# A hybrid diffusion block on one core: a new order of the modulation stage, and a Fourier stage on folded tokens

## The reference

```python
mod_x = silu(c) @ w_ada + b_ada                      # shift, scale, gate: 3 x 2048
mod_c = silu(c_ctx) @ w_ada + b_ada
h_x = rmsnorm(x, g_pre) * (1 + sc_x) + sh_x
h_c = rmsnorm(ctx, g_pre) * (1 + sc_c) + sh_c
xa, ba, ca, za, u, zb, f, zc, gl = split(h_x @ w_in)
u_c = h_c @ w_in[:, u columns]
...                                                  # conv branch, state-space branch
def fourier_mix(f):                                  # 4 groups of 256 channels
    fg = f.reshape(1, 512, 4, 256)
    return fft2(fg, axes=(1, 3), norm='ortho').real.reshape(1, 512, 1024)
yc = ((fourier_mix(f) @ fourier_w) * silu(zc)) @ proj_c
m = g0 * ya + g1 * yb + g2 * yc                      # g = sigmoid(gl)
out = x + gate * rmsnorm(m @ w_out, g_post)
```

## Time and profile before

| | |
|---|---|
| median of 3 runs | 2119.97 us (2119.87 to 2121.78) |
| the profiled execution | 2119.78 us, its span 2118.0 us |
| TensorE busy | 2051.6 us, 97% of the span |
| DVE busy, ACT busy | 1086.1 us (51%), 586.1 us (28%) |
| modulation stage | 0 to 166 us |
| Fourier stage | 1484.5 to 1542.5 us |

### The profile page before, as it was taken

One profiled execution on the slowest core, in us unless ns is written; L12 is line 12 of the kernel. 1 busy time (PEld: TensorE's weight loads), 2 busy tenths in 40 slices (PEclk: granted clock), 3 DMA queues, 4 the chain that ended last, 5 costly groups with the idle time before them and its releaser, 6 DMA issues.

```text
span 2118.0 us, 26445 instructions
## 1 busy us (share of the span) xinstructions
PE 2051.6 (97%) x9915; PEld 1667.9 (79%) x9915; DVE 1086.1 (51%) x1596; ACT 586.1 (28%) x816; POOL 27.3 (1%) x16
## 2 busy tenths in 40 slices
PE   3999999999999999999999999999999999999996
PEld 0578888888888788888888888888588888888885
DVE  5445898888888545554333444332343333333333
ACT  4325233333333322222222222222122222222231
POOL 0003100000000000000000000000000000000000
PEclk9999999999999999999999999999999999999998
DMA  9873533343333544443334444444033333334423
GB/s 371 309 217 112 171 101 100 92 104 98 104 99 108 165 125 141 128 136 106 99 97 134 141 131 125 126 132 146 10 94 95 100 99 91 97 99 158 169 93 116
DMA packets 384830, 272.16 MB, mean 128 GB/s; under 512 B 24804, under 2 KB 349900, under 8 KB 382916
## 3 DMA queue, kind: packets, MB, share of 16 engines
q1 hardware_dynamic: 374416, 267.04, 40.9%
q10 hardware_dynamic: 10356, 4.35, 1.5%
HBM read 253.25 MB, written 18.09 MB: 128 GB/s over the span
## 4 chain that ended last, share of the span: by engine, by line
PE 80%; DVE 9%; DMA 4%; ACT 2%; ACTq 2%; issue 2%; SPq 0%; DVEq 0%
PE ac L704 20%; PE ac L705 20%; PE ac L708 20%; ACTq L1090 2%; DVE S L1549 2%; DMA M<-Tl 1%; PE ss L879 1%; PE ac L878 1%; PE ac L879 1%; PE ss L880 1%; PE ac L880 1%; PE ss L878 1%; ACT S L894 1%; DMA wslot<-w_in 1%; PE ac L845 1%
## 5 line engine op out<-in xcount | busy, mean ns | idle before, releaser
L1448 DVE TENSOR_TENSOR wlo<-wslot,whi 128x1024 fp32r<-128x1024 f32 x310 | 379.6, 1225 | 647.9 <-ACT whi L894 643.8
L894 ACT ACTIVATE whi<-wslot 128x1024 fp32r<-128x1024 f32 x328 | 347.1, 1060 | 1253.2 <-PE ac L708 1034.4
L704 PE MATMUL ac<-hxh,whi 128*128 128x512 f32 x1664 | 652.3, 392 | 0.0
L705 PE MATMUL ac<-hxl,whi 128*128 128x512 f32 x1664 | 648.0, 389 | 0.0
L708 PE MATMUL ac<-hxh,wlo 128*128 128x512 f32 x1664 | 411.1, 389 | 0.9 <-DVE wlo L1448 0.9
L704 PEld LDWEIGHTS ac<-hxh,whi 128*128 128x128 f32 x1664 | 312.4, 188 | 67.8 <-issue 3.1
L708 PEld LDWEIGHTS ac<-hxh,wlo 128*128 128x128 f32 x1664 | 312.3, 188 | 66.1 <-DVE wlo L1448 1.3
L705 PEld LDWEIGHTS ac<-hxl,whi 128*128 128x128 f32 x1664 | 312.5, 188 | 64.3 <-issue 0.2
L704 PE MATMUL ac<-bah,whi 128*128 128x512 f32 x384 | 149.4, 389 | 0.0
L705 PE MATMUL ac<-bal,whi 128*128 128x512 f32 x384 | 149.4, 389 | 0.0
L708 PE MATMUL ac<-bah,wlo 128*128 128x512 f32 x384 | 94.8, 389 | 0.0
(11 more groups left out here) (316 smaller groups left out, 2135.7 us busy)
## 6 DMA issues: line engine op xcount, KB each, us to landing
wslot<-w_in SPq DMA_DIRECT2D x224, 512.0 KB, 3.9
ring<-w_ada SPq DMA_DIRECT2D x64, 512.0 KB, 8.0
gwt<-w_ada SPq DMA_DIRECT2D x128, 128.0 KB, 2.4
wslot<-w_out SPq DMA_DIRECT2D x32, 512.0 KB, 3.6
wslot<-proj_a SPq DMA_DIRECT2D x16, 512.0 KB, 4.1
wslot<-proj_b SPq DMA_DIRECT2D x16, 512.0 KB, 4.0
wslot<-proj_c SPq DMA_DIRECT2D x16, 512.0 KB, 3.9
xn<-x SPq DMA_DIRECT2D x4, 1024.0 KB, 8.8
```

The source lines that it names most:

```text
L704: mm(ac[:, bank, :], w, xh, start=(v == 0 and q == 0), stop=False)
L705: mm(ac[:, bank, :], w, xl, start=False, stop=False)
L894: cp = lambda o, i, scale=1.0: nc.scalar.activation(o, i, ACT.Copy, scale=scale)
L1448: tt(wlo[:, s, :], wslot[:, s, :], whi[:, (U0[k] + j) % 2, :].bitcast(F32), ALU.subtract)\
```

## The change

Modulation stage: c and c_ctx are loaded first on SP's queue into `crow` and transposed alone; the other vectors are transposed behind `ada(3)`. On ACT's queue lam and log_dt come first. All these buffers leave the place of `whi`. DVE takes the token scales behind the sine, puts the zero-order hold (`zoh`) into quarter 0 and the powers (`chunk_powers`) behind it. Pieces of `w_ada` are spread between x and context pieces, SP issues weight units and ctx between pieces, and in DVE's loop each `low` comes before the next `modulate`.

Fourier stage: cosines are even and sines odd about token 256. As each `fT` tile appears, DVE folds it: token t plus token 512-t goes to `fP` (with token 0), their difference stays in `fT`; token 256 is treated apart (`p256`, with the signs `alt`). `channels` multiplies the sums with the cosine columns and the differences with the sine columns; `tokens` makes 257 cosine and 256 sine results of 256 folded tokens. The mix forms both halves of the 512 tokens, the second half written in reverse; ACT casts the high parts. Tables shrink to 1283 columns.

```diff
-V_BADA, V_GPRE, V_CONV, V_C, V_CC, V_END = 0, 32, 48, 72, 88, 104
+V_BADA, V_GPRE, V_CONV, V_END = 0, 32, 48, 72
...
-    r = Region(whi_at)
+    r = Region(abr_at + 4 * TC * 4)
+    crow = r("crow", [2 * KD, 128])
     vrow = r("vrow", [V_END, 128])
     lam = r("lam", [128, 2, P])
     ldt = r("ldt", [128, 1])
     zt = [r(f"zt{i}", [128, P]) for i in range(8)]
     ei = r("ei", [128, P], I32)
-    assert r.p <= hxl_at
+    assert r.p <= abr_at + KD // 2 * TC * 4
...
-    dftt = at("dftt", [128, 2, TT, T], bal_at)
+    dftt = at("dftt", [128, 5 * HT + 3], bal_at)
+    cosT = dftt[:, 0:2 * HT + 2].rearrange("p (k c) -> p k c", k=2)
+    sinT = dftt[:, 2 * HT + 2:4 * HT + 2].rearrange("p (k c) -> p k c", k=2)
+    alt = dftt[:, 4 * HT + 2:5 * HT + 3]
+    fP = at("fP", [128, KW, HT], bal_at + KW * T * 4 - KW * HT * 4)
...
+    p256 = at("p256", [FG, FG, FGW // 2 + 1], bal_at + 5152)
+    p256n = at("p256n", [FG, 128], bal_at + 5152 + 2080)
...
+        for n, src in enumerate((c[0:1, :], c_ctx.rearrange("(a n) -> a n", a=1))):
+            sp.dma_start(crow[n * KD:(n + 1) * KD, :], src.rearrange("a (r p) -> (a r) p", p=128)).then_inc(cv_in, 16)
         for t in range(TT):
             sp.dma_start(xn[:, t, :], x[0, t * 128:(t + 1) * 128, :]).then_inc(x_in[t], 16)
-        for n in range(8):
+        for n in range(32):
             ada_unit(n)
-            if n == 5:
-                first_unit(0)
-                first_unit(1)
-        for t in range(CT):
-            sp.dma_start(cn[:, t, :], ctx[0, t * 128:(t + 1) * 128, :]).then_inc(c_in, 16)
-        for q in range(1, 4):
-            for r in range(8):
-                ada_unit(8 * q + r)
-                if r == 3:
-                    first_unit(2 * q)
-                    first_unit(2 * q + 1)
+            if n % 8 >= 6:
+                first_unit(n // 8 * 2 + n % 2)
+            if n in (8, 9):
+                sp.dma_start(cn[:, n - 8, :], ctx[0, (n - 8) * 128:(n - 7) * 128, :]).then_inc(c_in, 16)
...
-        pe.wait_ge(vec_in, 96)
-        tr(ss[:, 0, 0:V_END], vrow[:, :], ident[0:V_END, 0:V_END])
-        tr(ss[:, 1, 0:G], drow[:, :, :].rearrange("n l h -> n (l h)"), ident[0:G, 0:G]).then_inc(vec_ps, 1)
+        pe.wait_ge(cv_in, 32)
+        tr(ss[:, 0, 0:2 * KD], crow[:, :], ident[0:2 * KD, 0:2 * KD]).then_inc(cv_ps, 1)
...
+            if n == 3:
+                pe.wait_ge(vec_in, 64)
+                tr(ss[:, 1, 0:V_END], vrow[:, :], ident[0:V_END, 0:V_END])
+                tr(ss[:, 1, 128:128 + G], drow[:, :, :].rearrange("n l h -> n (l h)"), ident[0:G, 0:G]).then_inc(vec_ps, 1)
         turn(0, 0)
         cols(0)
         for n in range(1, 4):
             turn(0, n)
+        for r in range(4):
+            x_piece(0, r, range(4))
+            ada(8 + r)
+        ada(12)
+        turn(0, 4)
+        ada(13)
+        turn(0, 5)
+        ada(14)
         for q in range(3):
-            for r in range(4):
-                ada(8 * q + 8 + 2 * r)
-                ada(8 * q + 9 + 2 * r)
-                x_piece(q, r, range(4))
-                if r // 2 == (0 if q else 1):
-                    turn(q, 4 + r % 2)
+            if q:
+                x_piece(q, 0, range(4))
+                ada(8 * q + 12)
+                x_piece(q, 1, range(4))
+                turn(q, 4)
+                ada(8 * q + 13)
+                x_piece(q, 2, range(4))
+                ada(8 * q + 14)
+                turn(q, 5)
+                x_piece(q, 3, range(4))
+            ada(8 * q + 15)
+            c_piece(q, 0)
             cols(q + 1)
-            for r in range(4):
+            turn(q + 1, 0)
+            for r in range(1, 4):
                 c_piece(q, r)
+                if q < 2:
+                    ada(8 * q + 15 + r)
                 turn(q + 1, r)
+            if q < 2:
+                ada(8 * q + 19)
...
+            pe.wait_ge(fold_done, 2 * gr + 2)
+            for t in range(2):
+                for parts, c0, c1 in ((fP, 0, 129), (fT[:, :].rearrange("p (k t) -> p k t", t=T), 129, FGW)):
+                    for q in range(2):
+                        last = mm(ss[:, gr, t * FGW + c0:t * FGW + c1], parts[:, 2 * gr + q, t * 128:(t + 1) * 128],
+                                  dftw[:, q, c0:c1], start=(q == 0), stop=(q == 1))
+            last.then_inc(p_ps, 1)
+
+        def tokens(gr):
+            pe.wait_ge(p_cp, gr + 1)
+            b = 2 * (gr % 2)
             if gr >= 2:
+                pe.wait_ge(ac_free[b], A0[6] // 4 + 1)
+            for t in range(2):
+                mm(ac[:, b, 0:HT + 1], pp[:, gr, t, 0:128], cosT[:, t, :], start=(t == 0), stop=False)
+            mm(ac[:, b, 0:HT + 1], p256[0:FG, gr, 0:128], alt[0:FG, :], start=False, stop=True).then_inc(pw_done, 1)
+            if gr >= 2:
+                pe.wait_ge(ac_free[b + 1], A0[6] // 4 + 1)
+            for t in range(2):
+                last = mm(ac[:, b + 1, 0:HT], pp[:, gr, t, 128:FGW], sinT[:, t, :], start=(t == 0), stop=(t == 1))
+            last.then_inc(pw_done, 1)
+
+        for gr in range(FG):
+            if gr == FG - 1:
+                pe.wait_ge(fold_done, KW)
+                middle = fT[:, :].rearrange("p (g q t) -> p g q t", q=2, t=T)
                 for q in range(2):
+                    last = mm(ac[0:FG, 3, 0:129], middle[:, :, q, HT], dftw[:, q, 0:129], start=(q == 0), stop=(q == 1))
+                last.then_inc(tok_ps, 1)
+            channels(gr)
+        pe.wait_ge(tok_cp, 2)
         for gr in range(FG):
+            tokens(gr)
+            if gr == 0:
+                pe.wait_ge(p_cp, FG)
+                for t in range(2):
+                    mm(ss[:, 0, 0:HT + 1], p128[:, t, :], cosT[:, t, :], start=(t == 0), stop=False)
+                mm(ss[:, 0, 0:HT + 1], p256n[:, :], alt[0:FG, :], start=False, stop=True).then_inc(y128_ps, 1)
...
+        for i, src in enumerate((lam_re, lam_im)):
+            act.dma_start(lam[:, i, :], src[0].rearrange("d g p -> (d g) p")).then_inc(ssm_in, 16)
+        act.dma_start(ldt[:, :], log_dt[0].rearrange("d (g a) -> (d g) a", a=1)).then_inc(ssm_in, 16)
+        for rr, src in ((V_BADA, b_ada[0:1, 0:2 * D]), (V_GPRE, g_pre[0:1, :]), (V_CONV, conv_w)):
             n = src.shape[0] * src.shape[1] // 128
             act.dma_start(vrow[rr:rr + n, :], src.rearrange("a (r p) -> (a r) p", p=128)).then_inc(vec_in, 16)
         act.dma_start(drow[:, :, :], ssm_d.rearrange("a (n h) -> (a n) h", h=H).unsqueeze(1).to_broadcast([G, L, H]))\
            .then_inc(vec_in, 16)
-        for i, src in enumerate((lam_re, lam_im)):
-            act.dma_start(lam[:, i, :], src[0].rearrange("d g p -> (d g) p")).then_inc(ssm_in, 16)
-        act.dma_start(ldt[:, :], log_dt[0].rearrange("d (g a) -> (d g) a", a=1)).then_inc(ssm_in, 16)
-        act.wait_ge(vec_cp, 1)
-        a(small[:, 0:32], vecs[:, V_C:V_END], ACT.Sigmoid).then_inc(sg_done, 1)
+        act.wait_ge(cv_ps, 1)
+        a(small[:, 0:32], ss[:, 0, 0:32], ACT.Sigmoid).then_inc(sg_done, 1)
...
-        act.wait_ge(zn_done, 1)
+        high(0, 0)
         hi_first(0)
-        high(0, 0)
+        high(0, 1)
+        high(0, 2)
         hi_first(1)
-        for n in range(1, 4):
-            high(0, n)
+        high(0, 3)
...
+        for gr in range(FG):
+            if gr == FG - 1:
+                act.wait_ge(tok_ps, 1)
+                for g in range(FG):
+                    last = cp(p256[:, g, :], ac[0:FG, 3, 0:129], ident[0:FG, g:g + 1])
+                last.then_inc(tok_cp, 1)
+                act.wait_ge(tok_cp, 1)
+                cp(p256n[:, :].rearrange("p (g c) -> p g c", c=32)[:, :, 0], p256[:, :, 128]).then_inc(tok_cp, 1)
+            act.wait_ge(p_ps, gr + 1)
+            half = ss[:, gr, :].rearrange("p (t c) -> p t c", c=FGW)
+            cp(pp[:, gr, :, 0:128], half[:, :, 0:128])
+            cp(pp[:, gr, :, 129:FGW], half[:, :, 129:FGW])
+            cp(p128[:, :, 32 * gr:32 * gr + 1], half[:, :, 128:129]).then_inc(p_cp, 1)
+        for gr in range(FG):
+            act.wait_ge(pw_done, 2 * gr + 1)
             if gr:
+                act.wait_ge(gs_free, gr)
+            cp(gsig[:, 0:HT + 1], ac[:, 2 * (gr % 2), 0:HT + 1]).then_inc(ac_free[2 * (gr % 2)], 1)
+            for n, y in enumerate((gt, gtm2)):
+                act.wait_ge(mix_y, 2 * gr + n + 1)
+                cp(b2nd[:, 2 * gr + n, 0, :], y[:, :]).then_inc(mix_hi, 1)
...
             modulate(q, 0)
+            low(q, 0)
             modulate(q, 1)
-            low(q, 0)
+            low(q, 1)
             lo_first(2 * q)
             modulate(q, 2)
-            low(q, 1)
+            low(q, 2)
             modulate(q, 3)
-            low(q, 2)
+            low(q, 3)
             lo_first(2 * q + 1)
-            low(q, 3)
             if q == 0:
+                zoh()
                 token_scale(TT, CT, 2)
-            modulate(q, 4)
-            low(q, 4)
-            modulate(q, 5)
-            low(q, 5)
+            for n in range(4, 6):
+                modulate(q, n)
```

(80 more changed lines are left out.)

97 lines of the change are left out of this document (36 added, 61 removed).

## The result

The changed kernel took 2101.19 us (median of four runs, 2100.96 to 2102.53), the kernel before 2120.09 on the same chip (2119.87 to 2121.78): a ratio of 0.9911 (0.9896 to 0.9927). That is 18.9 us faster. I had forecast 2089.2, a gain of 30.6 on the profiled execution of before; sign and order were right, the gain is two thirds of it, and the time lies 3.2 us above the range.

What follows compares the result with a forecast made beforehand. The prediction took TensorE, busy for 97% of the span, as the bound. From the profiled 2119.78 us it took 26.8 (Fourier stage) and 3.8 (modulation stage), giving 2089.2 us, range 2084 to 2098.

Steps and rivals of the forecast that it cites:

- What binds, and the sign: Whole kernel: TensorE binds, so only fewer of its cycles or pauses help; faster by over 4 us, chance 0.97.
- Fourier term: Fourier stage: TensorE's records fall from 44.96 to 17.7 us, and the product on b2nd starts 26.8 us sooner.
- channel step: Fourier stage: 64 records of 129 or 127 columns at 0.116 us each, 7.4 us where it was 13.8.
- token records: Fourier stage: 40 records at 0.216 us, 8.6 us for 27.5, and 6 for channel 128, 1.3 for 3.4.
- Loads at the start, DVE's and ACT's vectors: Modulation stage start: vectors cost no wait, first modulated tile at 44.2 us, 4.9 us gained by the first quarter.
- First quarter: Modulation stage: piece 15 waits some 1.4 us, powers covered but for 0.1; gain 3.8 us at the second quarter.
- Second and third quarter: Modulation stage, its quarters 1 and 2: same TensorE work, most idling goes, gain grows to 5.0 us.
- Last quarter: Modulation stage: DVE's serial chain makes TensorE pause 1.3 and 2.4 us, costing 2.1 us.
- The stage's sum: Modulation stage: net gain 2.9 to 4.6 us, taken as 3.8, with ends 0 and 7.2.
- Rival 4: Fourier stage: new hand-overs bring TensorE's lower clock and double its 17.7 us, 2107 us; chance 0.04.
- Rival 2: Modulation stage gives nothing: the serial tile chain and emptied ring take back 6.2 us, 2093 us; chance 0.13.
- Rivals 1, 3 and 5: Mix binds the Fourier stage, 2093.5 us (0.16); modulation gives 7, 2086 (0.09); reversed passes slow, 2133 (0.02).

Runs made afterwards that it cites:

- run 8: Changed kernel with the middle token's matmuls over 128 partitions (zeros in the rest) instead of 4; a single execution, span 2099.5 us.
- run 4: Changed kernel with useless matmuls put into TensorE's waits in the modulation stage, no wait removed; 2096.53 us.
- run 6: Changed kernel with the first quarter's pieces taken two by two and DVE's old loop order (low part behind the next tile's modulation); 2096.14 us.
- Run 9: The kernel of run 6 with chunk_powers moved ahead of the context tiles on DVE; 2091.85 us.
- kernel 1: Fourier part of the change alone, the modulation stage as in the kernel before; 2095.32 us.
- 13: The kernel of Run 9 with the middle token's matmuls over 128 partitions instead of 4, without useless matmuls; 2091.76 us.
- run 5: Changed kernel with the first quarter's w_ada pieces taken two by two ahead of each x piece, as before the change; 2098.35 us.
- kernel 7: kernel 3 with TensorE's old order in all quarters, DMA and ACT orders still changed; 2098.28 us.
- kernel 3: Changed kernel with DVE's old loop order, each low part behind the next tile's modulation; 2096.87 us.

## Why the prediction was off

- **What binds, and the sign:** right.
- **Fourier term, -26.8 forecast, -25.4 measured.** The channel step (0.111 us a record for 0.116), the mix, b2nd ready at 28.3 and the absence of a wait there were right, and so was the covering product. The term that was mis-sized is that of the token records: "40 x 0.216" and "6 x 0.216" took no notice that ten of these 46 multiply over 4 partitions. They took 11.74 us for 9.9; run 8 shows 9.8 us once they are 128 deep. Of these 1.8 us some 0.4 are hidden by waits for a bank that I forecast and that did not come.
- **Loads at the start, DVE's and ACT's vectors:** no wait for the vectors, as forecast, and a gain of 4.6 us at the first quarter's start for 4.9. That the two agree so well is luck. Piece 7's matmuls end at 42.0 us, 1.1 us later than forecast and 0.7 us later than before the change, so the first modulated tile comes 5.2 us sooner and not 6.2; the chain of transposes and tiles behind it was put 0.7 us too long.
- **First quarter: the step that failed.** "Piece 15 waits some 1.4 us for its load" was 2.82 us, and the lower clock from there on cost another 2.75 (run 4), a term that the sum did not have. I had written that the powers are covered "but for 0.1": true in the changed kernel, since TensorE was late, and 2.76 us as soon as it was not (run 6). Run 9 has the forecast gain of 3.8 us at this place to the tenth, but with pairs, the old loop order and the powers moved; it shows that the stage has these 3.8 us to give, not that the steps of my forecast were right.
- **Second and third quarter:** TensorE is full as forecast, but the gain did not grow from there by the 1.2 us that I added: 29.3 us for the second quarter against 29.5, and for the same work 16.5 us for the third against 16.2. A piece alone costs 0.98 us where two together cost 1.83, 0.07 more each, 0.5 us in a quarter; the rest is open.
- **Last quarter, -2.1 forecast, -3.8 measured.** The two pauses were sized well (3.3 us for 3.7). Behind the second the clock was at its lower level for 3.4 us, which makes the 1.6 or 1.7 us that are missing (run 4 took 1.6 of them back).
- **The stage's sum** has a slip of its own: the steps add up to 5.0 - 2.1 = 2.9 us, the lower end of "2.9 to 4.6", and I took 3.8.
- **Rival 4, the clock, was the right mechanism in the wrong place and with too small a chance (0.04).** I looked for it in the Fourier stage's hand-overs, and took the earlier trace rows (a pause of 1.83 us, hardly a loss) as evidence against it. That was one execution: runs 1, 4, 6 and 13 show the same pause with the fall. The Trainium skill (TensorE: Matmul & The Clock Gate, The HAM clock gate) has an idle array fall to half rate. The traces show such falls, at 0.50 for 3.4 to 10.2 us with pauses of 1.9 to 3.1 us, but not at every such pause: there is none in run 5, at 2.76 us. I had priced it only as a doubling of one whole stage and not as a surcharge on each wait that the change makes. The modulation stage's own waits, which I forecast almost rightly, were where it belonged.
- **Rival 2** ("gives nothing", 2093) came closest in direction, but the stage gave less than nothing. **Rivals 1, 3 and 5** are refuted: b2nd is 4.5 us early, the stage lost, and reversed passes cost 0.41 us.

The 12.0 us between forecast and result can be divided by the marks in the traces. The clock takes 4.8: 2.75 in the first quarter, 0.4 at its start, some 1.6 in the last. Piece 15's longer wait is 1.4, and 1.0 more is lost in the first quarter: some 0.5 by single pieces, the rest is open. The second and third quarter lack 1.2. The Fourier stage lacks 1.4, the start 0.3, the slip in the sum 0.9, and 0.8 is the drift between the stages. That is 11.8. The clock's part is the one that an edit shows most directly: run 4 fills the waits, leaves the work as it is and takes 4.7 us back, 3.8 of them within the stage.

## What to carry to other kernels

Price a wait on a busy TensorE as the wait and what the clock takes behind it: here a 2 to 3 us pause cost another 1.6 us or more, in some executions and not in others, and matmuls that compute nothing won it back. When a wait goes, look at what it covered before counting the gain: the same 5.4 us of DVE work was free behind one wait and cost some 3 us without it. And an order on one queue is right only with the orders on the others: kernel 7 (2098.28 us) was slower than kernel 3 (2096.87), from which it differs in TensorE's order alone, and than kernel 1 (2095.32), where all orders of the stage are the old ones.
